# Causal convolution of a Conformer layer on TensorE: four tiles as two output phases on 64-row blocks and one by diagonals, changed to six tiles as four output phases on 32-row blocks

## What is computed

```python
def causal_depthwise_conv(x, w):
    k, c = w.shape
    return lax.conv_general_dilated(
        x, w[:, None, :].astype(x.dtype), window_strides=(1,), padding=[(k - 1, 0)],
        dimension_numbers=("NWC", "WIO", "NWC"), feature_group_count=c)

def mixer_conformer_conv(x, w_pw1, b_pw1, w_dw, b_dw, ln_g, ln_b, w_pw2):
    h = x @ w_pw1 + b_pw1
    a, g = jnp.split(h, 2, axis=-1)
    h = a * jax.nn.sigmoid(g)
    h = causal_depthwise_conv(h, w_dw) + b_dw
    h = jax.nn.silu(layer_norm(h, ln_g, ln_b))
    return h @ w_pw2
```

## Time and profile before

| | us |
|---|---|
| median of 3 runs | 2545.72 (2544.5 to 2546.34) |
| the profiled execution | 2546.59 |
| its span in the trace | 2544.8 |
| convolution on TensorE, layer 0 | 101.4 to 165.9 |
| convolution on TensorE, layer 3 | 2003.5 to 2068.3 |

### The profile page before, as it was taken

One profiled execution on the slowest core, in us unless ns is written; L12 is line 12 of the kernel. 1 busy time (PEld: TensorE's weight loads), 2 busy tenths in 40 slices (PEclk: granted clock), 3 DMA queues, 4 the chain that ended last, 5 costly groups with the idle time before them and its releaser, 6 DMA issues. The chain is left out here.

```text
span 2544.8 us, 41246 instructions
## 1 busy us (share of the span) xinstructions
PE 2520.1 (99%) x17241; PEld 2314.1 (91%) x17241; DVE 1955.3 (77%) x2571; ACT 1200.0 (47%) x1960; POOL 1.4 (0%) x10
## 2 busy tenths in 40 slices
PE   9999999999999999999999999999999999999999
PEld 7899999889888899998898899998898999999888
DVE  6988999577454679995784479996677979999576
ACT  6775444436233254443362245444356766444335
POOL 0000000000000000000000000000000000000000
PEclk9999999999999999999999999999999999999999
DMA  5202333324322223333233224333222203333322
GB/s 156 73 12 92 113 103 108 103 88 128 95 92 91 84 89 103 107 101 108 82 101 97 94 67 123 103 108 107 92 91 93 66 26 97 103 107 102 108 82 76
DMA packets 267054, 240.10 MB, mean 94 GB/s; under 512 B 14908, under 2 KB 212852, under 8 KB 266740
## 3 DMA queue, kind: packets, MB, share of 16 engines
q1 hardware_dynamic: 266292, 236.94, 30.2%
q10 hardware_dynamic: 576, 0.52, 0.1%
HBM read 233.21 MB, written 2.10 MB: 92 GB/s over the span
## 5 line engine op out<-in xcount | busy, mean ns | idle before, releaser
L1786 DVE TENSOR_TENSOR w_lo<-raw,w_hi 128x1024 fp32r<-128x1024 f32 x287 | 345.4, 1222 | 266.0 <-ACT w_hi L1309 265.7
L1309 ACT CAST w_hi<-raw 128x1024 fp32r<-128x1024 f32 x287 | 294.8, 1045 | 372.8 <-DMA raw<-in_ffn_w_down_dram 104.1
L879 PE MATMUL psum<-h_hi,w_lo 128*128 128x512 f32 x872 | 341.4, 392 | 0.0
L881 PE MATMUL psum<-h_hi,w_hi 128*128 128x512 f32 x872 | 339.4, 389 | 0.0
L880 PE MATMUL psum<-h_lo,w_hi 128*128 128x512 f32 x856 | 333.2, 389 | 0.0
L1024 PE MATMUL psum<-a_hi,w_lo 128*128 128x256 f32 x1088 | 280.9, 286 | 6.6 <-DVE w_lo L1786 5.1
L1024 PE MATMUL psum<-a_hi,w_hi 128*128 128x256 f32 x1088 | 277.5, 284 | 0.0
L1190 PE MATMUL psum<-h_hi,w_hi 128*128 128x256 f32 x768 | 217.3, 283 | 0.0
L1191 PE MATMUL psum<-h_hi,w_hi 128*128 128x256 f32 x768 | 217.3, 283 | 0.0
L1024 PEld LDWEIGHTS psum<-a_hi,w_lo 128*128 128x128 f32 x1088 | 209.1, 192 | 8.7 <-DVE w_lo L1786 4.6
L1024 PEld LDWEIGHTS psum<-a_hi,w_hi 128*128 128x128 f32 x1088 | 209.3, 192 | 0.3
(11 more groups left out here) (362 smaller groups left out, 6494.3 us busy)
## 6 DMA issues: line engine op xcount, KB each, us to landing
raw<-in_ffn_w_gate_dram SPq DMA_DIRECT2D x176, 256.0 KB, 3.0
raw<-in_ffn_w_up_dram SPq DMA_DIRECT2D x176, 256.0 KB, 3.3
raw<-in_ffn_w_down_dram SPq DMA_DIRECT2D x176, 256.0 KB, 3.1
raw<-in_a_w_pw_dram SPq DMA_DIRECT2D x94, 256.0 KB, 3.1
raw<-in_ple_w_gate_dram SPq DMA_DIRECT2D x64, 256.0 KB, 3.2
raw<-in_b_w_in_dram SPq DMA_DIRECT2D x64, 256.0 KB, 3.0
raw<-in_c_w_in_dram SPq DMA_DIRECT2D x48, 256.0 KB, 2.9
raw<-in_b_w_out_dram SPq DMA_DIRECT2D x32, 256.0 KB, 3.1
```

Source lines behind the costliest of these rows:

```text
L879: pe.matmul(bank(grp.g, j), st_lo, mv_hi, start=(k == 0), stop=False, skip_group_check=by_tiles(grp))
L881: done = pe.matmul(bank(grp.g, j), st_hi, mv_hi, start=False, stop=(ku == last and a == UK - 1), skip_group_check=by_tiles(grp))
L1309: act.copy(hi_u[u % RING], raw_u[u % RING]).then_inc(hi_ready, 1)
L1786: dve.tensor_tensor(lo_u[u % RING], raw_u[u % RING], hi_u[u % RING].bitcast(F32), ALU.subtract)\
```

## The change

Tiles 2 to 7 (`QUADS`) are now all convolved on TensorE by four output phases. The stationary operand is a block of 32 input channels by 128 columns (32 output channels for each of four neighbouring tokens). A tile has four row groups of 32 channels, each with a PSUM bank of its own, and 34 steps (`STEPS` = 31 + 3). Tiles 2 to 5 are done whole, with 128 moving columns; tiles 6 and 7 in two token halves with 64 columns, in the order (6, first), (7, first), (6, second), (7, second): eight segments, alternating between two sets of four banks. The diagonals, the DMAs that turned phases, VectorE's taps of tiles 2, 3 and 7 and the `conv_begin` steps go. In their place each segment has 16 copies from one group of 32 partitions in PSUM to another in SBUF: eight on VectorE (row groups 0 and 1) and eight on ScalarE (2 and 3). ScalarE makes the blocks of tiles 2 and 3 as before; VectorE makes those of tiles 4 to 7 with two instructions a tile. `centre` stands after step 20 of segment 3 as two matmuls of 256 columns, `conv_stats(s, 0)` after step 18 of segment 7.

```diff
+PHASES = 4
+ROWS = P // PHASES
+STEPS = TAPS_A + PHASES - 1
...
+QUADS = (2, 3, 4, 5, 6, 7)
+ACT_BLOCKS = 2
+A_BLOCKS = 3
+SEGMENTS = ((0, None), (1, None), (2, None), (3, None), (4, 0), (5, 0), (4, 1), (5, 1))
...
+CENTRE_IN, CENTRE_AT = 3, 20
+STATS_AT = 18
...
+        def moves(s, i, groups):
+
+            n, (v0, n_v) = SEGMENTS[i][0], segment_span(i)
+            y = by_phase(tiles(h_f32, CONV_Y + QUADS[n]))
+            return [(rows(y, r)[:, PHASES - 1 - j, v0:v0 + n_v], rows(segment_bank(s, i, r), j))
+                    for r in groups for j in range(PHASES)]
+
+        HIGH, LOW = (2, 3), (0, 1)
...
-            def phase_tap(s, n, e):
-
-                at = e % 2 * (CW // 2) + e // 2
+            def quad_tap(s, i, e):
+
+                n, (v0, n_v) = SEGMENTS[i][0], segment_span(i)
+                at = e % PHASES * (CW // PHASES) + e // PHASES + v0
                 for w, x in ((0, 1), (1, 0), (0, 0)):
-                    for r in range(2):
-                        moving = conv_split(n, x)[r * TILE_ROWS:(r + 1) * TILE_ROWS, at:at + HALF]
-                        last = pe.matmul(phase_bank(s, n, r)[:, 0:HALF], block_pair(n, e, w, r), moving,
-                                         start=(e == PHASED[n][1] and (w, x) == (0, 1)),
-                                         stop=(e == TAPS_A and (w, x) == (0, 0)))
+                    for r in range(PHASES):
+                        moving = rows(conv_split(n, x), r)[:, at:at + n_v]
+                        block = rows(tap_blocks(n, w), r)[:, e * ROWS:e * ROWS + P]
+                        last = pe.matmul(segment_bank(s, i, r), block, moving, start=(e == 0 and (w, x) == (0, 1)),
+                                         stop=(e == STEPS - 1 and (w, x) == (0, 0)))
                 return last
...
+                for i, (n, h) in enumerate(SEGMENTS):
+                    if i < 2:
+                        take_half(s.taps_g + i)
+                    else:
+                        pe.wait_ge(moved_high, moved(s, i - 2))
+                        pe.wait_ge(moved_low, moved(s, i - 2))
+                    if i == CENTRE_IN + 1:
+                        pe.wait_ge(centre_saved, c + 1)
...
+                    for e in range(STEPS):
+                        last = quad_tap(s, i, e)
+                        if i == CENTRE_IN and e == CENTRE_AT:
                             centre(s)
-                    last.then_inc(taps_done, 1)
...
+                        if i == len(SEGMENTS) - 1 and e == STATS_AT:
+                            conv_stats(s, 0)
                     last.then_inc(taps_done, 1)
...
+            def move(s, i):
+
+                act.wait_ge(taps_done, moved(s, i))
+                for y, out_of in moves(s, i, HIGH):
+                    last = act.copy(y, out_of)
+                last.then_inc(moved_high, 1)
...
+                move(s, 6)
+                load_sqrt()
+                half_moments(s, 0)
+                half_root(s, 0)
+                move(s, 7)
+                load_silu()
+                conv_half_square(s, 6)
+                half_affine_pair(s, 0, 0)
+                half_affine_pair(s, 0, 1)
+                conv_half_square(s, 7)
...
+            def move_low(s, i):
+
+                dve.wait_ge(taps_done, moved(s, i))
+                for y, out_of in moves(s, i, LOW):
+                    last = dve.tensor_copy(y, out_of)
+                last.then_inc(moved_low, 1)
...
+            def make_blocks(s, n):
+
+                if n >= A_BLOCKS:
+                    dve.wait_ge(pe_done, s.groups[-1].end())
+                m = QUADS[n]
+                for part in range(2):
+                    taps = (taps_lo if part else prm_taps(s)).rearrange("p (k m) -> p k m", m=DT)[:, :, m:m + 1]
+                    last = dve.tensor_tensor(three(tap_block(n, 0, part, TAPS_A), TAPS_A), many(rep[:, :], TAPS_A),
+                                             taps.broadcast_to([P, TAPS_A, ROWS]), ALU.mult)
+                last.then_inc(blocks_made, 1)
...
+                own.add(dve.tensor_tensor(sum_sq, tiles(tmp, 0), tiles(tmp, 1), ALU.add))
+                move_low(s, 3)
+                wait_moved(s, 3)
+                place_centred(s, 5)
```

More of the change, by code:

```diff
@@ L381, in tap_block @@
[L381 to L401, removed]
+            return ap.rearrange("p (q v) -> p q v", q=PHASES)
@@ L403, in prm_taps, with mean_bank, square @@
+        def mean_bank(s):
+            return bank(s.taps_g, 0, 2).rearrange("p (h s) -> p h s", h=2)[:, :, SEQ // PHASES:SEQ // PHASES + HALF]
+        SQUARES = DT + TILES
+        def square(m):
+            return tiles(a_f32, SQUARES + m - TILES)
         def prm_taps(s):
@@ L587, in trunk @@
         taps_done = sem("taps_done")
[L588 removed]
+        moved_high = sem("moved_high")
+        moved_low = sem("moved_low")
         no_blocks = sem("no_blocks")
[L590 to L592 removed]
         proj_sq = sem("proj_sq")
@@ L916, in centre @@
             def centre(s):
+                pe.wait_ge(moved_high, moved(s, CENTRE_IN - 1))
+                pe.wait_ge(moved_low, moved(s, CENTRE_IN - 1))
                 pe.wait_ge(ysum_ready, s.layer // 3 + 1)
-                pe.matmul(bank(s.taps_g + 1, 0), ones_r[:, :], ysum[:, :], start=True, stop=True).then_inc(centre_done, 1)
+                for h in range(2):
+                    last = pe.matmul(mean_bank(s)[:, h], ones_r[:, :], hcol(ysum, h), start=True, stop=True)
+                last.then_inc(centre_done, 1)
             def conv_stats(s, h):
+                pe.wait_ge(moved_high, moved(s, len(SEGMENTS) - 2 + h))
                 pe.wait_ge(conv_sums, 4 * (s.layer // 3) + 2 * h + 1)
@@ new lines, in conv_bias, with conv_tile, centre_sum @@
+            def conv_bias(s, m):
+                return col("a_b_dw", s.layer // 3, m)
+            def conv_tile(m, n=1):
+                return tiles(h_f32, CONV_Y + m, n)
+            def centre_sum(s):
+                move_low(s, 0)
+                move_low(s, 1)
+                own.settle()
+                wait_moved(s, 0)
+                wait_moved(s, 1)
+                for m in range(2):
+                    own.add(dve.scalar_tensor_tensor(tiles(tmp, 4 + m), conv_tile(2 + m), conv_bias(s, 2 + m), conv_tile(m),
+                                                     ALU.add, ALU.add))
@@ L2254, in convolve @@
                         lo_to(min(lo_end[0] + 1, lo_end_at))
-                    for m in (m0, m0 + 1) if k > first or not begun else ():
+                    for m in (m0, m0 + 1):
                         x = conv_x[:, m, PAD - taps + 1 + k:PAD - taps + 1 + k + SEQ]
```

443 lines of the change are left out of this document (170 added, 273 removed).

## The result

| | before | after |
|---|---|---|
| median of 4 runs, us | 2545.11 (2543.06 to 2546.34) | 2713.49 (2710.29 to 2716.69) |
| span of the profiled execution, us | 2544.8 | 2714.6 |
| its mean granted clock | 0.999 | 0.964 |
| convolution on TensorE, layer 0, us | 64.5 | 135.4 (101.7 to 237.1) |
| convolution on TensorE, layer 3, us | 64.8 | 135.0 (2095.9 to 2230.9) |

The changed kernel is slower by 6.6%: the ratio is 1.0662, interval 1.0644 to 1.0681. I had forecast 2615 us and a range up to 2700. In the changed kernel the four-phase matmul is line 932, the mixer's is line 1000, the first `a_hi` line 1442, and the feed-forward matmuls of 512 columns, formerly at lines 879 to 881, are lines 868 to 870.

The account below looks back on a forecast made before the run. TensorE, busy 99% at full clock, was taken as the bound, its new stream paced by weight loads. Two layers of 31.4 us convolution plus 3.0 us stage end add 68.8 us: 2615 us forecast, range 2592 to 2700.

Parts of the forecast that it names:

- rival 4: Convolution on TensorE: clock at 1.2 GHz as the array streams under half of each group, 2660 us; chance 5%.
- the end of the stage: Last tap to first mixer matmul: ScalarE's copies, table load and square in a row, +3.0 us a layer, bounds 1.5 and 5.
- The main term: Convolution on TensorE: 816 groups at 0.116 us, paced by weight loads, 96.0 us against 64.6, +31.4 us a layer.
- Rival 1: Convolution on TensorE: streaming sets the pace, groups 0.067 us whole and 0.040 half, kernel faster at 2525 us; chance 12%.
- rival 3: Convolution on TensorE: loads of four row groups go two by two, 0.22 us a group, 2785 us; chance 7%.
- Rival 2: Convolution on TensorE: instruction issue sets the pace, deciding from 0.015 us each, up to 0.165 us a group, 2695 us; chance 18%.
- The edits costed at nothing: Convolution: waits for copies and `centre_saved`, blocks on VectorE, removed taps, `conv_begin`, diagonals and turning DMAs, all put at nothing.
- The tight wait: Segment 5 needs ScalarE's `move_low(s, 3)`, about 9 us after segment 3 ends against 11.8 available; holds by 3 us.
- rival 5: Whole kernel: no change within 0.2%, at a pace of 0.072 to 0.079 us a group; chance 3%.

Follow-up runs that it names:

- e8: Kernel before, with all steps but first and last of the four phased tiles streaming 64 columns instead of 256: 2613.89 us, one execution.
- e1: Changed kernel with the half segments streaming all 128 columns of their tile, copies still taking their half: 2638.87 us, ratio 1.0365.
- e9: e5 with every four-phase matmul streaming its 128 columns twice, same loads and instructions: 2624.0 us, ratio 1.0309.
- e4: Kernel before with h_hi, h_lo and what lies behind them moved by 128 bytes in SBUF, no instruction changed: 2566.79 us, ratio 1.0083.
- e2: e1 with ScalarE loading its SiLU table before its eight last copies instead of behind them: 2635.92 us, ratio 1.0355.
- e6: e5 with only row groups 0 and 1 issued in steps 1 to 32 of segments 0 to 3: 2769.71 us, one execution.
- e7: e5 with loads of 64 instead of 128 stationary columns in steps 1 to 32 of segments 0 to 3: 2659.07 us, one execution.
- e5: e2 with a 32-word pad behind `rep`, putting h_hi and h_lo back where the kernel before had them: executions of 2675.63, 2734.38, 2735.34 and 2736.66 us.
- e10: Changed kernel with only the 32-word pad behind `rep`, h_hi and h_lo back in their old place: 2716.11 us, ratio 1.0702.

## Why the prediction was wrong

**The step that failed** is rival 4, "the stage runs at 1.2 GHz". I gave it 5% because the granted clock never left 1.00 in any stage. That row could not speak to the question. Its slices are 64 us long and a 9 means 90% or more, so it hides short falls; the trace has one of 3.4 us at 238.2, in layer 0's mixer. And nearly all of the kernel before streams about as long as it loads or longer, 256 columns or 512 behind a load of 128, so the new ratio of streaming to loading had no row in a stream of any length. I named the narrow stream as the reason, and took the absence of rows for evidence against it. What the runs showed: with 64 columns the clock fell to 0.50 for 95.6 us in each layer. It was tested by e8 (before, narrowed: it falls), e1 (halves widened: it holds in seven of eight stages) and e9 (doubled: it holds in all eight).

**Its price was also too low.** I took 0.17 us a group at 1.2 GHz from the start of the run. Measured it is 0.213: load and pace double with the clock. `conv_stats` took about 1 us longer. The mixer's start ran at half clock too, but that cost almost nothing: from its first matmul to the first of 512 columns it is 92.7 us (242.16 to 334.87) against 92.3 before. A layer lost 37 us by the clock (74.9 / 2, below) and not 22. Even my rival's 2660 would have missed.

**A term was missing**: the place of `h_hi` and `h_lo`. I read the edit of `a_end` only as room for `rep`. It costs 22 us (e4).

The miss in sum: 2713.5 against 2614.5 are 99 us. The clock is 2713.5 - 2638.6 = 74.9 (the median of e1's three executions with the clock held), the place 2566.8 - 2544.6 = 22.2, together 97.1; 1.9 are left, about what the end of the stage took above its term, 2 x (4.1 - 3.0).

**What held.** The main term, the pace at full clock: 0.116 predicted for a group, 0.111 between starts and 0.117 with the stops; the stage 96.0 predicted, 96.5 and 97.5 in layer 3 of e1 and e2, at full clock. That the load sets the pace of a burst is shown from two sides, by e6 (half of the instructions, the same 0.112) and e7 (half of the load, 0.064). Rival 1 (streaming) and rival 3 (loads in twos) are out: four loads start together, and half the columns gain nothing. Rival 2 was nearer than I thought: issue doesn't set the pace of a burst (e6), but the supply of 0.015 to 0.016 us an instruction (e7) is where I said it would decide. The end of the stage: eight copies took 2.17 us (1.9 by the estimate), the table 1.28 and the square in full, 5.1 us against 1.05 before. That is +4.1 us a layer, against the +3.0 of the sum and within its bounds. That the table was in the way is shown by e2's 1.4 us a layer. The edits costed at nothing cost next to nothing in waits: in all of the changed kernel's trace TensorE's waits at L932 are 1.5 us on issue and 0.3 on a copy of VectorE's, none of any size in front of segment 5, and the waits for the statistics are gone.

**Smaller errors.** The tight wait was not that of segment 5 but that of segment 2, in layer 0. I had VectorE with nothing else to do beside the blocks; it was busy for 23.07 of the first 23.20 us, with the splitting of weights among others, and began the copies of segment 0 only at 121.96. Rival 1's sum is zero at 0.074 us a group by its own terms, not 0.075 (64.6 - 1.3 - 3.0 = 60.3 us, against the 61.4 named), and the range leaves out rival 5, no change, besides 1 and 3.

**What stays open.** Why the same instructions lose the clock in one stage of eight with the tensors in one place (e2) and in seven of eight in another (e5); the longer stop in front of segment 2 is a candidate that no run tried alone. Why two row groups of 128 columns lost it within 3 us (e6), where four held it for at least 24. And why 128 bytes of offset cost a 512-column matmul 5 ns.

None of these kernels beats the one before, and the count gives the reason: a tile in two phases is 96 pairs at 0.120 us, 11.5 us; in four phases it is 102 groups at 0.111, 11.3 us, and each half segment costs as much as a whole one. Besides, TensorE now does the taps of tiles 2, 3 and 7 that VectorE had done beside it.

## What to carry over

Count weight loads before columns: splitting a matmul into more row groups saved nothing here, where each group still brings a new set of 128-column weights. When a change shortens what is streamed behind each load, price the stage at 1.2 GHz as well, all of it and what follows, and don't take a clean clock row of a kernel with longer streams as evidence against. Look at where a changed buffer size moves its neighbours. And a clock row in tenths by slice doesn't say that the clock never fell; windows do.

## What the hardware did that I had not expected

- The clock fell to 1.2 GHz in the middle of a stream without gaps: at 153.0, in segment 4, for 95.6 us. Streams of 64 columns behind loads of 128 lost it in both layers of the changed kernel and of e8; of 128 columns on four row groups, in some stages (e1, e2, e5, e10), in the profiled ones each time within 3.5 us of the start of a stop of 0.5 to 1.0 us; of 256, in none of e9's eight.
- At 1.2 GHz the load of 128 columns paces at 0.213 us, against 0.111.
- A 512-column fp32r matmul takes 232 ns instead of 227 when `h_hi` and `h_lo` lie 128 bytes further on (e4).
- Over tens of us TensorE's instructions came at 0.015 to 0.016 us each, though a burst of e7 ran at half of that (0.064 for eight).
- Eight copies of 32x64 from PSUM across quadrants take 2.17 us on ScalarE, 0.27 each.
